# Modulation weights and x in two feature halves, with six of sixteen weight tiles multiplied on TensorE

## What is computed

```python
cond = jax.nn.silu(c)
mod = (cond @ w_ada[l] + b_ada[l])[:, None, :]
sh1, sc1, gt1, sh2, sc2, gt2 = jnp.split(mod, 6, axis=-1)
h = x * (1 + sc1) + sh1
p = h @ w_in[l]
```

## Time and profile before

| | us |
|---|---|
| median of 3 runs | 1051.26 (1050.17 to 1055.8) |
| profiled execution | 1055.53 |
| its span | 1053.8 |

### The profile page before, as it was taken

How to read it: one execution, slowest core, us unless ns; L and a number is a source line. 1 busy time by engine, 2 the same in 40 slices (tenths; PEclk the granted TensorE clock), 3 DMA queues, 4 the chain that set the end, 5 groups by cost and what they waited for, 6 DMA issues and landing times.

```text
span 1053.8 us, 27460 instructions
## 1 busy us (share of the span) xinstructions
PE 969.4 (92%) x11539; PEld 806.5 (77%) x11539; DVE 677.1 (64%) x925; ACT 474.3 (45%) x579; POOL 381.2 (36%) x222
## 2 busy tenths in 40 slices
PE   1998889999989999899899999798999999999993
PEld 1776677777768678667688888688899898998993
DVE  7325567668837867664222255468778788787887
ACT  0546344346435633434532242274545446455451
POOL 8332510411240131123554445245153352451542
PEclk9998998999999999999999999889999999999997
DMA  9332234234332333332344337222341442423201
GB/s 362 119 98 68 81 87 141 55 91 124 93 82 84 96 96 101 103 109 61 121 120 110 107 112 230 70 61 81 94 146 40 120 119 60 139 80 97 63 1 81
DMA packets 122967, 108.10 MB, mean 103 GB/s; under 512 B 5411, under 2 KB 104657, under 8 KB 122865
## 3 DMA queue, kind: packets, MB, share of 16 engines
q1 hardware_dynamic: 112768, 83.44, 26.4%
q10 hardware_dynamic: 10097, 23.16, 7.2%
HBM read 100.23 MB, written 2.10 MB: 97 GB/s over the span
## 4 chain that ended last, share of the span: by engine, by line
PE 74%; DVE 15%; ACT 3%; issue 3%; DMA 2%; POOL 2%; SPq 1%; ACTq 0%; DVEq 0%; POOLq 0%
PE set L2247 13%; PE bank L1882 11%; PE bank L2333 7%; PE set L2333 7%; PE set L2186 6%; PE bank L2186 5%; PE set L1936 4%; PE set L2285 3%; PE bank L2247 2%; PE set L1924 2%; PE set L1948 2%; PE bank L1863 2%; DVE y L1502 1%; PE set L1960 1%; DVE Q L1276 1%
## 5 line engine op out<-in xcount | busy, mean ns | idle before, releaser
L663 POOL TENSOR_TENSOR w_lo<-w_raw,w_hi 128x1024 fp32r<-128x1024 f32 (+2 forms) x75 | 171.2, 2282 | 388.0 <-ACT w_hi L773 379.4
L773 ACT ACTIVATE w_hi<-w_raw 128x1024 fp32r<-128x1024 f32 (+2 forms) x81 | 81.8, 1010 | 103.9 <-PE set L2186 35.2
L822 ACT ACTIVATE Q<-set 128x1024 f32<-128x1024 f32 x56 | 57.5, 1026 | 134.4 <-PE set L1936 68.9
L1882 PE MATMUL bank<-h_hi,w_hi 128*128 128x512 f32 x256 | 108.7, 425 | 3.4 <-POOL w_lo L663 3.3
L1152 ACT ACTIVATE w_hi<-w_raw 128x1024 fp32r<-128x1024 f32 x70 | 74.3, 1062 | 81.2 <-PE set L2247 64.3
L1614 DVE SCALAR_TENSOR_TENSOR res<-set,mod,res 128x256 f32<-128x256 f32 x192 | 92.9, 484 | 25.2 <-PE set L2247 16.5
L2247 PE MATMUL set<-a_hi,w_hi 128*128 128x256 f32 x384 | 108.9, 284 | 0.0
L2247 PE MATMUL set<-a_hi,w_lo 128*128 128x256 f32 x384 | 108.6, 283 | 0.0
L2247 PE MATMUL set<-a_lo,w_hi 128*128 128x256 f32 x384 | 108.6, 283 | 0.0
L1882 PE MATMUL bank<-h_lo,w_hi 128*128 128x512 f32 x256 | 104.2, 407 | 0.2 <-issue 0.2
L1882 PE MATMUL bank<-h_hi,w_lo 128*128 128x512 f32 x256 | 103.6, 405 | 0.0
(11 more groups left out here) (361 smaller groups left out, 2322.8 us busy)
## 6 DMA issues: line engine op xcount, KB each, us to landing
w_raw<-in_w_ff_dram SPq DMA_DIRECT2D x64, 512.0 KB, 3.9
w_raw<-in_w_in_dram SPq DMA_DIRECT2D x46, 512.0 KB, 3.7
y<-in_w_ada_dram ACTq DMA_DIRECT2D x20, 512.0 KB, 3.7
ada<-in_w_ada_dram SPq DMA_DIRECT2D x16, 512.0 KB, 10.3
Q<-in_w_ada_dram ACTq DMA_DIRECT2D x12, 512.0 KB, 3.7
w_raw<-in_w_rwkv_up_dram SPq DMA_DIRECT2D x8, 512.0 KB, 3.6
w_raw<-in_w_out_dram SPq DMA_DIRECT2D x8, 512.0 KB, 4.5
xtok<-in_x_dram SPq DMA_DIRECT2D x4, 512.0 KB, 6.7
```

Source lines behind the costliest of these rows:

```text
L663: link(pool.tensor_tensor(part_of(k, w_lo), raw_part(k), part_of(k, w_hi).bitcast(F32), ALU.subtract), "lo_ready")
L773: link(act.activation(part_of(k, w_hi), raw_part(k), ACT.Copy), "hi_ready")
L822: link(act.activation(by_half(tile), psum_flat(set_of(name)), ACT.Copy), "act_kept")
L1882: mm = pe.matmul(o, w, hx, start=(m == 0), stop=(m == 3 * KT - 1))
```

## The change

The features of sh1, sc1 and x are split into two halves of 512. Half 0 of everything is loaded first, `mod` and `h` of half 0 are made, chunks 0 and 1 take their products with half 0, and half 1 follows.

- A tile of `w_ada` is now 256 rows (a `pair` of 128) by 512 columns, still 512 KB; the order is half, then section (scale, shift), then pair: tiles 0 to 7 are half 0, 8 to 15 half 1.
- DVE adds ten of the sixteen tiles, each with two operations of 128x512. The other six (2, 3, 6, 7 of half 0; 11, 15 of half 1) go to PE, which multiplies each with the columns of silu(c): 8 products with one moving column each (`multiply_ada`), straight into the PSUM columns where the sums over partitions land (`multiply_sum`).
- SP loads: 8 tiles, chunks 0 and 1, half 0 of x, 8 tiles, half 1 of x.
- `x_bank` uses banks 2 to 5 alone, four feature tiles at a time.
- DVE puts its sums of half 1 between the four `h_lo` of half 0.
- PE: half 0's modulation, 16 transposes, four tiles' products of chunk 0, then a tile of `w_ada`, products of chunk 1, sums, another tile, sums, 16 transposes, and the last four tiles.
- POOL splits chunks 0 and 1 between its two rounds of constants.

```diff
+        ADA_TILES = [(half, sec, pair) for half in range(2) for sec in range(2) for pair in range(4)]
+        BY_PRODUCT = [pair >= 2 + half for half, sec, pair in ADA_TILES]
...
-            return bank[(2, 3, 4, 5, 0, 1)[f % 6]]
+            return bank[2 + f % 4]
...
+            for q in range(KT):
+                load_first_ada(q)
             for k in range(2):
                 load_chunk(sp, k)
-            for j in range(TB):
-                sp.dma_start(xtok[:, j, :], x[0, j * P:(j + 1) * P, :]).then_inc(sem(f"x_in{j}"), 16)
+            load_x(0)
+            for q in range(KT, 2 * KT):
+                load_first_ada(q)
+            load_x(1)
...
             for z in range(2):
                 half = slice(z * C, (z + 1) * C)
+                if z == 1:
+                    split_lo(0)
+                    split_lo(1)
...
-            act.wait_ge(sem("mod_ready"), 3)
             for f in range(KT):
+                if f % 4 == 0:
+                    act.wait_ge(sem("mod_ready"), 3 * (f // 4 + 1))
...
+            def sum_ada(q):
+                half, sec, pair = ADA_TILES[q]
                 dve.wait_ge(sem(f"ada_in{q % NADA}"), 16 * (q // NADA + 1))
+                total = acc[:, sec, half * S:(half + 1) * S]
+                for i in range(2):
+                    kt, part = 2 * pair + i, ada[q % NADA][:, i * S:(i + 1) * S]
...
+            for q in (0, 1, 4, 5):
+                sum_ada(q)
+            parameters()
+            first_modulation(0)
+            sum_ada(8)
+            for f, q in enumerate((9, 10, 12, 13)):
+                h_low(f)
+                sum_ada(q)
+            sum_ada(14)
+            first_modulation(1)
+            for f in range(4, KT):
+                h_low(f)
...
+            def multiply_ada(q, first=False):
+                half, sec, pair = ADA_TILES[q]
+                pe.wait_ge(sem(f"ada_in{q % NADA}"), 16 * (q // NADA + 1))
+                for i in range(2):
+                    for f in range(4):
+                        to = 8 * sec + 4 * half + f
+                        mm = pe.matmul(bank[1][:, to:to + 1], ada[q % NADA][:, i * S + f * P:i * S + (f + 1) * P], der(CS + 2 * pair + i),
+                                       start=first and i == 0 and f == 0, stop=False, skip_group_check=True)
+                mm.then_inc(sem("ada_multiplied"), 1)
...
+            multiply_ada(2, True)
+            multiply_ada(3)
             pe.wait_ge(sem("params_in"), 16 * 15)
...
+            multiply_sum(0, 0, 2)
+            multiply_ada(6)
+            multiply_ada(7)
+            multiply_sum(0, 1, 4).then_inc(sem("mod_done"), 1)
...
+            turn_x(0)
...
+            for f in range(4):
+                feed_first(f)
+                feed_first_low(f)
+            multiply_ada(11)
+            feed_second(0)
+            feed_second(1)
+            multiply_sum(1, 0, 7)
+            feed_second(2)
+            multiply_ada(15)
+            multiply_sum(1, 1, 10).then_inc(sem("mod_done"), 1)
+            feed_second(3)
+            turn_x(1)
             LAG = 2
-            for f in range(KT + LAG):
+            for f in range(4, KT + LAG):
```

More of the change, by code:

```diff
@@ L542, in _, with load_first_ada, load_x @@
         def _(sp):
-            for q in range(2 * KT):
-                sec, kt = (1, 0)[q // KT], q % KT
+            def load_first_ada(q):
+                half, sec, pair = ADA_TILES[q]
                 if q >= NADA:
-                    sp.wait_ge(sem("ada_used"), q - NADA + 1)
-                sp.dma_start(ada[q % NADA][:, :], w_ada[0, kt * P:(kt + 1) * P, sec * D:(sec + 1) * D]).then_inc(sem(f"ada_in{q % NADA}"), 16)
+                    if BY_PRODUCT[q - NADA]:
+                        sp.wait_ge(sem("ada_multiplied"), sum(BY_PRODUCT[:q - NADA + 1]))
+                    else:
+                        sp.wait_ge(sem("ada_used"), q - NADA + 1 - sum(BY_PRODUCT[:q - NADA + 1]))
+                first = (1, 0)[sec] * D + half * S
+                src = w_ada[0, 2 * pair * P:2 * (pair + 1) * P, first:first + S].rearrange("(i p) f -> p i f", p=P)
+                sp.dma_start(ada[q % NADA][:, :].rearrange("p (i f) -> p i f", i=2), src).then_inc(sem(f"ada_in{q % NADA}"), 16)
+            def load_x(half):
+                for j in range(TB):
+                    sp.dma_start(xtok[:, j, half * S:(half + 1) * S],
+                                 x[0, j * P:(j + 1) * P, half * S:(half + 1) * S]).then_inc(sem(f"x_in{half}_{j}"), 16)
+            for q in range(KT):
+                load_first_ada(q)
             for k in range(2):
                 load_chunk(sp, k)
-            for j in range(TB):
-                sp.dma_start(xtok[:, j, :], x[0, j * P:(j + 1) * P, :]).then_inc(sem(f"x_in{j}"), 16)
+            load_x(0)
+            for q in range(KT, 2 * KT):
+                load_first_ada(q)
+            load_x(1)
             for k in range(2, RING):
@@ L659, in _ @@
             link(pool.memset(scanm[:, :].rearrange("p (c t) -> p c t", t=C)[:, :, 0:1], 0.0), "consts_ready")
[L661 to L665, removed]
+            for k in range(2, 5):
                 split_lo(k)
@@ L1233, in _ @@
-            for f in range(KT):
+                total = acc[:, sec, half * S:(half + 1) * S]
+                for i in range(2):
+                    kt, part = 2 * pair + i, ada[q % NADA][:, i * S:(i + 1) * S]
+                    if kt == 0:
+                        link(dve.tensor_scalar(total, part, der(CS), None, ALU.mult))
+                    else:
+                        link(dve.scalar_tensor_tensor(out=total, in0=part, scalar=der(CS + kt), in1=total, op0=ALU.mult, op1=ALU.add),
+                             "ada_used" if i else None)
@@ new lines, in first_modulation @@
+            def first_modulation(half):
+                scale, shift = slice(8 + 4 * half, 12 + 4 * half), slice(4 * half, 4 * half + 4)
+                dve.wait_ge(sem("mod_done"), half + 1)
+                link(dve.scalar_tensor_tensor(out=mod[:, scale], in0=bank[1][:, shift], scalar=1.0, in1=params[:, scale], op0=ALU.add, op1=ALU.add),
+                     "mod_ready")
+                link(dve.tensor_tensor(mod[:, shift], bank[1][:, scale], params[:, shift], ALU.add), "mod_ready")
+                link(dve.scalar_tensor_tensor(out=derived[:, NSH + 4 * half:NSH + 4 * half + 4], in0=bank[1][:, scale], scalar=-1.0,
+                                              in1=params[:, shift], op0=ALU.mult, op1=ALU.subtract), "mod_ready")
@@ L1234, in _, with h_low @@
+            def h_low(f):
                 dve.wait_ge(sem("h_unshifted"), f + 1)
@@ L1795, in _, with multiply_sum @@
             pe.transpose(bank[0][:, 2 * P:2 * P + KT], crow[:, :], ident[0:KT, 0:KT]).then_inc(sem("c_turned"), 1)
+            pe.wait_ge(sem("c_scaled"), 1)
+            def multiply_ada(q, first=False):
+                half, sec, pair = ADA_TILES[q]
+                pe.wait_ge(sem(f"ada_in{q % NADA}"), 16 * (q // NADA + 1))
[5 more added lines that the diff above has]
+                mm.then_inc(sem("ada_multiplied"), 1)
+            def multiply_sum(half, sec, used):
+                pe.wait_ge(sem("ada_used"), used)
+                for f in range(4):
+                    to = 8 * sec + 4 * half + f
+                    mm = pe.matmul(bank[1][:, to:to + 1], acc[:, sec, half * S + f * P:half * S + (f + 1) * P], ones_col[:, :],
+                                   start=False, stop=True, skip_group_check=True)
+                return mm
+            multiply_ada(2, True)
+            multiply_ada(3)
             pe.wait_ge(sem("params_in"), 16 * 15)
@@ L1802, in _, with turn_x @@
             pe.wait_ge(sem("ones_ready"), 1)
[L1803 to L1822, removed]
+            multiply_sum(0, 0, 2)
+            multiply_ada(6)
+            multiply_ada(7)
+            multiply_sum(0, 1, 4).then_inc(sem("mod_done"), 1)
+            def turn_x(half):
+                for j in range(TB):
+                    pe.wait_ge(sem(f"x_in{half}_{j}"), 16)
+                    for f in range(4 * half, 4 * half + 4):
+                        mm = pe.transpose(x_bank(f)[:, j * P:(j + 1) * P], xtok[:, j, f * P:(f + 1) * P], ident[:, :])
+                        if j == TB - 1:
+                            mm.then_inc(sem("x_turned"), 1)
+            turn_x(0)
             def terms_of(k, m):
@@ L1834, in first_chunk_part, with feed_first, feed_second, feed_first_low @@
                     mm.then_inc(sem("w_used"), 1)
+            def feed_first(f):
+                pe.wait_ge(sem("h_hi_ready"), f + 1)
+                pe.wait_ge(sem("lo_ready"), 1)
+                first_chunk_part(0, f, 0)
+                first_chunk_part(0, f, 2)
+            def feed_second(f):
+                pe.wait_ge(sem("lo_ready"), 2)
+                for term in (0, 2, 1):
+                    first_chunk_part(1, f, term)
+            def feed_first_low(f):
+                pe.wait_ge(sem("h_lo_ready"), f + 1)
+                first_chunk_part(0, f, 1)
```

(11 more changed lines are left out.)

5 lines of the change are left out of this document (4 added, 1 removed).

## The result

The changed kernel is slower: 1064.71 us in the median of 4 runs (1063.21 to 1068.2), against 1051.87 of before in the same comparison (4 runs, 1050.17 to 1055.8). The ratio is 1.0139, with a 95% interval of 1.0109 to 1.0169. The profiled execution took 1068.2 with a span of 1066.5, 12.7 more than the 1053.8 of before.

The account below looks back on a forecast made before the run. PE bounds the whole (92% busy), but the start up to chunk 2 decides: chunk 2 15.6 us later at the lower clock, less 2.0 for the block, gives +13.6; 1051.26 + 13.6 = 1064.9, range 1056.5 to 1069.

Parts of the forecast that it names:

- What decides: At the start: the change is worth its shift of the chain reaching chunk 2, 51.13 before; +13.6, passed through in full.
- The clock below a reading of 1.00: Before about 37 us TensorE runs at 1.2 GHz whatever the column says; one-column passes cost 0.221 us, not 0.101.
- Half 0: First half: PE's sums end at 26.05, first h_hi starts at 29.2 instead of 35.83, fourth h_lo ends at 38.6.
- The block: PE's two tiles, two sums and 12 chunk 1 products between the halves: 15.8 us at the lower clock, 2.0 taken off.
- h of half 1: Second half, at the lower clock: h_hi of tile 4 at 57.7, last h_lo ends at 64.8, chunk 2 at 66.7.
- The upper bound: Before chunk 2: with the clock low for the last 24 products too, they take 10.3 us; shift about +18.
- Loads and POOL: At the start: x loads hidden with 6 us and more to spare; POOL's split at 18.8 for 4.8 us also hidden.
- Rival B: Whole start at the upper clock: chunk 2 at 49.7, a shift of -1.4, about 1050; chance 0.10.
- Rival C: First half at the low clock, the rest high: chunk 2 at 57.5, +6.4, 1057.7; chance 0.17.
- Rival D: PE's next wait, around 82 us, takes up at most 2 us of the delay; no time of its own.

Follow-up runs that it names:

- `wide_128`: The changed kernel with the moving operand of every modulation product widened from 1 to 128 equal columns; ratio to before 1.0016, chunk 2 at 52.19.
- `dense_halves`: The changed kernel with all tiles on DVE, chunk 1 products between those of chunk 0, half 1's transposes ahead of its sums; ratio to before 0.998.

## Why the prediction was right

The forecast was 1064.9 and a shift of +13.6; measured were 1064.71 and 12.7 of span. The mechanism was the one forecast: one-column passes at the lower clock, in series on PE, twice in front of h. That the two totals agree to 0.2 us is luck; runs of one kernel differ by 5. Step by step:

- *What decides.* The start as its own regime, and the moment of chunk 2 as what the change is worth: the shift there is 14.27 (forecast 13.6), at the end of these two executions 12.7.
- *The clock below a reading of 1.00.* Right. Passes in the trace of after are 0.213 ((14.33 - 7.51) / 32), while the granted clock reads 1.00 (the row below). I had 0.221, since I divided the busy time of a batch, which also holds what the last pass takes beyond its 0.213 (16 passes at 0.213 are 3.41, the batch shows 3.54 and 3.57). Over 128 passes on the path that is 1.0 us too dear.

```profile
16.00:24.00 8.00, 8.00 (x39) 8.00 (x39) 0.80 (x5) 1.85 (x2) 6.43 (x10) 1.00 1.06 404
```

- *Half 0.* `mod` 25.7 (forecast 26.05 for the sums), h_hi 28.02 (29.2), fourth h_lo ends 37.24 (38.6). All in the order forecast, and early: by 80 passes at 0.008, by PE starting on tile 2 at 7.51 (7.66 forecast), and by each batch starting while the last pass of the one before still ends; h_lo 2.36 apart (2.34), but the last 2.10, since the first sum of a section is a short operation that I had counted long.
- *The block.* 37.88 to 53.25, 15.4 us; at the lower clock I had 15.8, and took 2.0 off because its 12 products of 512 columns might bring the clock up. That deduction is the step that failed: in the trace of after the twelve stand 0.43 apart (0.57 behind a batch of passes), all passes take 0.213, and nothing came off. Without it the forecast of chunk 2 would have been 66.7, 1.3 above the 65.40 measured, since the pass and half 0 were too dear; with it, it was 64.7, 0.7 below. Two errors of opposite sign hid each other.
- *h of half 1.* From 56.34, where h_hi of tile 4 starts, to chunk 2 are 9.06; forecast 2.40 + 4.71 + 1.92 = 9.03. The upper bound, with the clock low here too, did not come in this trace: products at 59 to 65 are 0.23 apart. It came in part in two of the runs: the 19 products in front of chunk 2 took 6.21 us with fills between the tiles, where they took 5.03 here. What decides between the two is open: the 16 transposes of half 1 stand in front of these fast products, but the 16 of half 0, from 24.89, were followed by products 0.43 apart.
- *Loads and POOL.* Hidden, as forecast. Chunks 0 and 1 were split by POOL from 16.95 to 21.74, needed at 29.45 (the first product with w_lo). Its constants, which I had at about 36, were done at 27.9.
- *Rival B*, the rule of the Trainium skill that activity releases the throttle ("TensorE: Matmul & The Clock Gate", "What's actually happening"): PE was busy from 7.51 to 28.5 without a break and every pass before the transposes took 0.213, so the trace does not agree with it for one-column products. With 128 columns the clock did come up, and rival B can be held against that run: chunk 2 came at 52.2 rather than the 49.7 I had for it. The last h_lo of half 0 was as priced (30.66 against 30.7); the block took 10.1 instead of 7.6, of which 1.5 is tile 11, slow again behind the thin stretch of h of half 0 (3.27 against 1.78 for tile 15), and the rest the dearer pass of 128 columns and the transposes' wait for `mod`.
- *Rival C* did not come: the clock stayed low through the block.
- *Rival D.* At the wait that I named nothing is given back: at 98.01, where the chain of before has 83.76, the shift is still 14.25. That the end shows 1.6 less is no more than single executions differ by.

The last point led to one more reading. POOL makes a diagonal matrix once in each of four passes of the scan (line 683 before, 705 after), which serves as a mark. It starts at 184.85, 274.96, 371.64 and 461.50 before and at 195.75, 286.25, 379.89 and 474.93 after, so the shift is 10.9, 11.3, 8.3 and 13.4 at these marks. Through the scan it wanders over 5 us, though nothing there was changed. The granted clock dips at other places in the two traces, which could do it; that it is the cause was not tested.

The profiled executions of the other runs say the same: from chunk 2 to the end, where all these kernels have the same work, they took between 993.7 us (1054.2 - 60.49, the products of chunk 1 behind the block) and 1002.7 (1053.8 - 51.13, the kernel before). So one pair of spans can't tell how much of a shift of 14 us reaches the end. Nor can the interval of the first comparison, 1.0109 to 1.0169 or 11.5 to 17.8 us: it holds 12.7 and 14.27 alike. Whether anything is given back stays open.

## What to carry to other kernels

In these traces a product with one moving column was paced by its stationary load (PEld, the load of that operand, is busy for all 8.00 us from 16 to 24 in the changed kernel), and TensorE's clock never came up over a run of them; price it at the slow pass, 0.213 here, unless dense products stand around it. Read the clock from the durations of a known operation: in the changed kernel the column read 1.00 from 7.51 to 56 us, and every pass, product and transpose there had the duration of 1.2 GHz. When work is moved to another engine, write down what stands behind it in that engine's order: six tiles cost 3.5 us beside the loads, and some 13 where they stood between two halves of h. An operand that is broadcast to more columns was the cheaper warm-up here, if its PSUM space is free: it took 13.2 us off the start, where five fills in front took 1.9 and fills between the passes nothing. It only won back what the change had lost; no variant is clearly faster than the kernel before.

## What the runs showed of the hardware

- The same 128x128 fp32 stationary loads with 1, 32 and 128 moving columns: 0.213, 0.213 and, once the clock was up, 0.112 us a pass. 128 columns cost hardly more than one (0.112 against 0.101 to 0.109 with the clock up), and the clock rose within the first 32 of them, where an unbroken run with 32 columns, from 7.73 to 25, did not bring it up.
- The clock stayed up over one-column passes when a product of 512 columns stood between each eight of them (0.101 a pass). Without, it held for 32 passes, was gone behind them and an idle 0.67 us, and one-column passes did not bring it back: granted 0.50 from 16 to 24, with PE busy throughout.
- In the same run (five fills in front) it came back while PE did nothing but transposes of 128x128: they begin at 23.50 and last 421 ns, the last of them 273 ns, and the granted clock goes from 0.50 to 1.00 at about 26.4. In the changed kernel 16 such transposes from 24.89 on stayed slow to the end. What the difference is was not tested.
- It fell behind waits of PE: in `wide_128`, with three products per 2.36 us of h of half 0 (0.55 from 24 to 32), and in `dense_halves` behind the 2.31 us for DVE's last tile (0.65 from 40 to 48). With six products per 2.36 us, as `dense_halves` has them in h of half 0, it stayed up (1.00 from 24 to 32, products 0.23 apart).
- Runs of one kernel differ more than in the first comparison: `dense_halves` had 1042.51 to 1053.06 in 12 runs. Changes of 2 to 3 us at the start are seen at once in the trace, at chunk 2, and hardly at all in the time.
